# Merge stage: the samples' gather on ScalarE's queue, and a first unit that multiplies its two column halves one after the other

## What is computed

```
xn = rms_norm(x, norm_in)
u = xn @ w_in                                  # columns for both mixers and the merge gates
o_a = rwkv7_mixer(u_a, ...)                    # (tokens, 1024)
o_b = nsa_mixer(q, gates, ...) * silu(g_b)     # (tokens, 1024)
gate_a, gate_b = split(sigmoid(u_m), 2)
merged = gate_a * (o_a @ w_pa) + gate_b * (o_b @ w_pb)
h = x + merged @ w_o
y = rms_norm(h, norm_out)
```

## Time and profile before

| | us |
|---|---|
| median of 3 runs | 2466.56 |
| lowest and highest | 2466.09, 2470.59 |
| the profiled execution, its own time | 2464.72 |
| its span in the profile | 2463.0 |

### The profile page before, as it was taken

How to read it: one execution, slowest core, us unless ns; L and a number is a source line. 1 busy time by engine, 2 the same in 40 slices (tenths; PEclk the granted TensorE clock), 3 DMA queues, 4 the chain that set the end, 5 groups by cost and what they waited for, 6 DMA issues and landing times. The chain is left out here.

```text
span 2463.0 us, 51947 instructions
## 1 busy us (share of the span) xinstructions
PE 2261.5 (92%) x21510; PEld 2082.4 (85%) x21510; DVE 1193.0 (48%) x2352; ACT 803.2 (33%) x1593; POOL 532.9 (22%) x398
## 2 busy tenths in 40 slices
PE   5999999899999989999999789899989869999996
PEld 4998888787888878899999778788987669999996
DVE  4343545445454545368887264444226425353223
ACT  4334233332323332222222345455223214232221
POOL 0000000000000000001100699999604420000000
PEclk8999999999999999999999899999989889999998
DMA  3321112212121121288675412321559955443232
GB/s 114 104 88 50 63 52 71 72 42 71 49 68 50 64 84 51 78 269 282 225 245 181 146 61 83 86 65 55 195 185 307 312 170 181 141 139 128 97 100 82
DMA packets 134590, 302.09 MB, mean 123 GB/s; under 512 B 26442, under 2 KB 54324, under 8 KB 132820
## 3 DMA queue, kind: packets, MB, share of 16 engines
q1 hardware_dynamic: 95236, 208.86, 25.7%
q0 software_dynamic: 15824, 54.71, 6.5%
q10 hardware_dynamic: 23296, 35.20, 4.4%
HBM read 261.48 MB, written 45.54 MB: 125 GB/s over the span
## 5 line engine op out<-in xcount | busy, mean ns | idle before, releaser
L178 PE MATMUL acc<-xh,w_hi 128*128 128x272 f32 x3008 | 675.5, 306 | 42.1 <-DVE w_lo L161 17.9
L178 PE MATMUL acc<-xl,w_hi 128*128 128x272 f32 x3008 | 632.1, 292 | 0.0
L178 PE MATMUL acc<-xh,w_lo 128*128 128x272 f32 x3008 | 631.9, 292 | 0.0
L178 PEld LDWEIGHTS acc<-xh,w_hi 128*128 128x128 f32 x3008 | 479.0, 193 | 101.0 <-issue 53.5
L178 PEld LDWEIGHTS acc<-xl,w_hi 128*128 128x128 f32 x3008 | 484.1, 193 | 0.0
L178 PEld LDWEIGHTS acc<-xh,w_lo 128*128 128x128 f32 x3008 | 481.1, 193 | 0.0
L161 DVE TENSOR_TENSOR w_lo<-w_raw,w_hi 128x1024 fp32r<-128x1024 f32 x164 | 200.6, 1223 | 422.0 <-ACT w_hi L153 421.1
L153 ACT ACTIVATE w_hi<-w_raw 128x1024 fp32r<-128x1024 f32 x188 | 198.4, 1055 | 295.3 <-PE acc L178 220.7
L1265 DVE SCALAR_TENSOR_TENSOR b_C<-b_rows,b_pos_s,b_C 128x512 f32<-128x512 f32 x240 | 162.4, 744 | 0.0
L2618 DVE TENSOR_TENSOR m_w_lo<-m_w,m_w_hi 128x1024 fp32r<-128x1024 f32 x64 | 78.4, 1224 | 164.2 <-ACT m_w_hi L2563 164.1
L970 PEld LDWEIGHTS rbank<-m 64*64 64x64 f32 x3840 | 120.2, 135 | 22.9 <-issue 14.1
(11 more groups left out here) (408 smaller groups left out, 3350.4 us busy)
## 6 DMA issues: line engine op xcount, KB each, us to landing
w_raw<-in_w_all SPq DMA_DIRECT2D x168, 512.0 KB, 3.5
b_rows<-in_cmp_rows SPq DMA_DIRECT2D x128, 256.0 KB, 3.8
m_w<-in_w_mo SPq DMA_DIRECT2D x64, 512.0 KB, 3.9
w_raw<-in_w_all ACTq DMA_DIRECT2D x20, 512.0 KB, 5.9
tmp_uT<-ub ACTq DMA_DIRECT2D x35, 272.0 KB, 4.0
m_gates<-tmp_uT SPq DMA_DIRECT2D x32, 272.0 KB, 2.7
d_ring<-in_sel_k SPq DMA_DIRECT2D x64, 128.0 KB, 4.4
d_ring<-in_sel_k POOLq DMA_DIRECT2D x64, 128.0 KB, 4.6
```

The source lines that it names most:

```text
L178: ins = self.nc.tensor.matmul(acc[:, c, 0:HALF], w[:, k % KH, :], x[:, k, c * HALF:(c + 1) * HALF], start=(k == 0 and m == 0), stop=(k == ...
```

## The change

In `attend_samples`, ACT issues the last store to `obS` ahead of the last two evacuations. In `merge_and_out`, the gather of the samples' `o_a` moves from POOL's to ACT's queue, ahead of the identity. ACT and DVE split the first 8 operand tiles for the 512 prompt columns without waiting for the samples, with weight half 0 first, half 1 ahead of k tile 3 and half 2 ahead of k tile 5; the samples' 32 columns of all 8 tiles are split together at the end. PE's unit 0 does its first column half (columns 0 to 271) over all k tiles, then turns the samples, waits for their low part, and does the second column half (272 to 543).

```diff
--- before.py
+++ after.py
@@ -2187,8 +2187,8 @@
                 out(("Tn", bp), PTn[:, :, :], bank[0:DEC_T, bank_of["Tn", bp], 0:2 * P].rearrange("p (k n) -> p k n", k=2))
                 for n in range(2, N_UNIT):
                     turned(bp, n)
+            store(N_BP - 1)
             background(SAMPLE_PIECES)
-            store(N_BP - 1)
             act.wait_ge(sent, 16 * N_BP)
             for j in range(2):
                 act.wait_ge(stored[j], 16 * ((W.s1 - W.s0 + 1 - j) // 2))
@@ -2534,8 +2534,6 @@
 
         @block.gpsimd
         def _(pool):
-            pool.dma_start(oa_s[:, :].rearrange("n (h d) -> n h d", h=16), A["oS"].rearrange("h n d -> n h d"))\
-                .then_inc(oa_s_in, 16)
             for b in range(DEC_B):
                 src = A["obS"][b // 2, (b % 2) * HD:(b % 2 + 1) * HD, :].rearrange("(g t r) d -> t g (r d)", g=G_KV, t=DEC_T)
                 pool.dma_start(ob_s[b * DEC_T:(b + 1) * DEC_T, :].rearrange("n (g x) -> n g x", g=G_KV), src)\
@@ -2553,6 +2551,8 @@
         @block.scalar
         def _(act):
             f = nc.scalar.activation
+            act.dma_start(oa_s[:, :].rearrange("n (h d) -> n h d", h=16), A["oS"].rearrange("h n d -> n h d"))\
+                .then_inc(oa_s_in, 16)
             act.dma_start(ident[:, :], A["ident"]).then_inc(ident_in, 16)
 
             def high_part(x):
@@ -2567,20 +2567,22 @@
                 f(gates[n % N_RING_M][:, :], gates[n % N_RING_M][:, :], ACT.Sigmoid).then_inc(gated, 1)
 
             def o_high(k):
-                f(o_hi[:, k, :], o_raw[:, k, :], ACT.Copy).then_inc(o_hi_done, 1)
+                cols = slice(0, SEQ if k < KW else NT)
+                f(o_hi[:, k, cols], o_raw[:, k, cols], ACT.Copy).then_inc(o_hi_done, 1)
 
             def square(c):
                 act.wait_ge(added, c + 1)
                 if c >= 2:
                     act.wait_ge(summed, c - 1)
                 f(sq[:, c % 2, :], h[:, c, :], ACT.Square).then_inc(squared, 1)
-            act.wait_ge(taken, 1)
             for k in range(KW):
                 if k % 4 == 0:
                     act.wait_ge(oa_in[k // 4], 16)
+                if k in (0, 3, 5):
+                    high_part((k + 1) // 2 - (k > 0))
                 o_high(k)
-                if k in (1, 3, 5):
-                    high_part((k - 1) // 2)
+            act.wait_ge(taken, 1)
+            f(o_hi[:, 0:KW, SEQ:NT], o_raw[:, 0:KW, SEQ:NT], ACT.Copy).then_inc(o_hi_done, 1)
             for n in range(UNITS):
                 for x in halves_of(n):
                     if n or x > 2:
@@ -2619,8 +2621,10 @@
                     .then_inc(w_lo_done, 1)
 
             def o_low(k):
-                dve.wait_ge(o_hi_done, k + 1)
-                v.tensor_tensor(o_lo[:, k, :], o_raw[:, k, :], o_hi[:, k, :].bitcast(F32), ALU.subtract).then_inc(o_lo_done, 1)
+                dve.wait_ge(o_hi_done, k + 1 if k < KW else k + 2)
+                cols = slice(0, SEQ if k < KW else NT)
+                v.tensor_tensor(o_lo[:, k, cols], o_raw[:, k, cols], o_hi[:, k, cols].bitcast(F32), ALU.subtract)\
+                    .then_inc(o_lo_done, 1)
 
             def silu_half(q):
                 dve.wait_ge(sig, q + 1)
@@ -2659,12 +2663,15 @@
                     merged(n)
                 else:
                     add_residual(n)
+            for k in range(KW):
+                if k in (0, 3, 5):
+                    low_part((k + 1) // 2 - (k > 0))
+                o_low(k)
             dve.wait_ge(tps, 1)
             v.tensor_copy(o_raw[:, 0:KW, SEQ:NT], turn[0][:, 0:KW * NS].rearrange("p (k n) -> p k n", n=NS)).then_inc(taken, 1)
-            for k in range(KW):
-                o_low(k)
-                if k in (1, 3, 5):
-                    low_part((k - 1) // 2)
+            dve.wait_ge(o_hi_done, KW + 1)
+            v.tensor_tensor(o_lo[:, 0:KW, SEQ:NT], o_raw[:, 0:KW, SEQ:NT], o_hi[:, 0:KW, SEQ:NT].bitcast(F32), ALU.subtract)\
+                .then_inc(o_lo_done, 1)
             for n in range(UNITS):
                 for x in halves_of(n):
                     if n or x > 2:
@@ -2717,7 +2724,7 @@
                 j = x % N_RING_M
                 for k in tiles:
                     if ready is not None:
-                        pe.wait_ge(ready, k + 1)
+                        pe.wait_ge(ready[0], k + 1 + ready[1])
                     for m, (a, b) in enumerate(((w_hi, x_hi), (w_hi, x_lo), (w_lo, x_hi))):
                         for c in range(2):
                             ins = mm(out[:, c, 0:HALF], a[j][:, k % KW, :], b[:, k, c * HALF:(c + 1) * HALF],
@@ -2732,9 +2739,23 @@
                              start=(c == 0), stop=(c == N_OUT - 1))
                 ins.then_inc(summed, 1)
             lower, upper = range(KW), range(KW, KD)
-            pe.wait_ge(ident_in, 16)
-            pe.wait_ge(oa_s_in, 16)
-            turn_samples(0, oa_s)
+
+            def first_unit():
+
+                pe.wait_ge(w_lo_done, 1)
+                for c in range(2):
+                    if c:
+                        pe.wait_ge(ident_in, 16)
+                        pe.wait_ge(oa_s_in, 16)
+                        turn_samples(0, oa_s)
+                        pe.wait_ge(o_lo_done, KW + 1)
+                    for k in lower:
+                        if c == 0:
+                            pe.wait_ge(o_lo_done, k + 1)
+                        for m, (a, b) in enumerate(((w_hi, o_hi), (w_hi, o_lo), (w_lo, o_hi))):
+                            ins = mm(acc[0][:, c, 0:HALF], a[0][:, k, :], b[:, k, c * HALF:(c + 1) * HALF],
+                                     start=(k == 0 and m == 0), stop=(k == KW - 1 and m == 2))
+                ins.then_inc(half_done, 1)
             for n in range(UNITS):
                 if n == TURN_AT:
                     pe.wait_ge(ob_s_in, 16 * DEC_B)
@@ -2747,10 +2768,12 @@
                     else:
                         pe.wait_ge(added, n - 1 - 2 * N_OUT)
                 out, x = acc[n % 2], first_half(n)
-                if n < 2 * N_OUT:
-                    half(x, out, lower if n < N_OUT else upper, o_hi, o_lo, True, True, o_lo_done if n in (0, N_OUT) else None)
+                if n == 0:
+                    first_unit()
+                elif n < 2 * N_OUT:
+                    half(x, out, lower if n < N_OUT else upper, o_hi, o_lo, True, True, (o_lo_done, 1) if n == N_OUT else None)
                 else:
-                    ready = m_lo_done if n == 2 * N_OUT else None
+                    ready = (m_lo_done, 0) if n == 2 * N_OUT else None
                     half(x, out, lower, m_hi, m_lo, True, False, ready)
                     half(x + 1, out, upper, m_hi, m_lo, False, True, ready)
                 c = n - 2 * N_OUT - 1
```

## The result

The change made the kernel slower. Over 7 runs each the median went from 2468.43 to 2476.79 us, a ratio of 1.004 (95% interval 1.003 to 1.005), and when it was timed once more beside its parts, from 2469.04 to 2475.91, 1.0034 (1.0022 to 1.0046). That is +8.4 and +6.9 us, where +6.6 was forecast. The median of before was 2466.56 over the three runs shown ahead of the forecast and 2466.6 to 2469.0 in later ones.

What follows compares the result with a forecast made beforehand. PE work bounds the kernel almost everywhere, with full DMA engines limiting the time before unit 0. Unit 0's 10.7 us delay, less 3.9 from the stall and 0.2 from the store, gives +6.6: 2473.2 us, range 2467.5 to 2477.5.

Steps and rivals of the forecast that it cites:

- the first term: Merge's first unit: with its new order, unit 0 ends and unit 1 begins 10.7 us late.
- step 2: Unit 0's first pass: late weight halves delay the operands, so its last three matmuls end at 2039.2.
- A: The forecast itself: late operands, serial turn, second pass at half clock; +6.6 us, range 2470.5 to 2476, chance 0.62.
- the store: End of the samples' stage: the last obS store issued ahead of the evacuations gains 0 to 0.4 us, taken as 0.2.
- Steps 4 and 5: Unit 0 after the turn: samples' copies and subtraction until 2044.1, then 24 matmuls at half clock, 5.4 us, until 2049.6.
- What the stall gives back: Ahead of and in unit 3: PE's 2.4 us idle time and the clock's fall go, returning 3.9 us.
- The gather: Merge start: on ACT's queue ahead of the identity, issue and landing cost nothing, as both are needed only at about 2039.
- Rival B: Unit 0's second pass: the clock is up in time, 3.0 us in place of 5.4; +4.1 us total, chance 0.20.
- A's tail: Unit 0's operands come 1 to 2 us earlier than forecast, so the slowdown stays within 0.2%; chance 0.04.
- same: Whole kernel: the measured time differs from before by no more than about 0.2%, 4.9 us; chance 0.27.
- Rival C: Unit 0's loads: weight half 1 lands sooner, at 2025.0, so the kernel is not slower, 2466.4 us; chance 0.08.
- Rival D: ACT's queue: work behind the samples' copy delays the product unit 2 needs; 2.6 us on the path, +9.2, chance 0.10.

Runs made afterwards that it cites:

- only_first_unit: The change without the moved store and with the gather back on POOL's queue, timed against the kernel before: 2474.02 us, ratio 1.0025.
- change_again: The changed kernel, unaltered, timed once more against the kernel before: 2475.91 us, ratio 1.0034.
- loads_and_gather: The kernel before with SP's two obN loads behind weight half 4 and the samples' gather on ACT's queue: 2464.87 us, ratio 0.9992 to the kernel before.
- fill_gap: The change with 24 useless matmuls ahead of k tile 3 and 6 ahead of k tile 5: 2475.08 us, ratio 1.003 to the kernel before.
- gates_late_warm: The kernel before with later obN and g_b loads, plus 20 useless identity products between the samples' turn and unit 0: 2464.72 us, ratio 0.999.

## Why the prediction came close, and where it was off

- **What failed** is the size of the first term, the 10.7 us by which unit 0 is late: it was 11.6. Most of the miss lies in step 2, the end of the first pass, forecast at 24.6 us from SP's first load and measured at 25.2. Measured 2476.79 lies inside the whole range, but above A's own, 2470.5 to 2476. The rest of the distance to 2473.2 lies outside the merge, in the base and in the start, which the sum gave no room but the 0.2 of the store.
- **The mechanism held, step by step.** PE's first matmul was forecast 3.4 us earlier and came at 12.1 us from SP's first load, before 15.5. It stopped behind the ninth, for 5.5 us. The turn came serially at half clock (3.62 us), then the samples' steps, then 24 matmuls at half clock. only_first_unit has the same late unit 1 and the same merge.
- **The sum.** Unit 1 was forecast 10.7 us late; it came 11.6 late (35.86 less 24.25), and 11.2 in change_again. The missing 0.9 lies in step 2 with 0.6: weight half 2 landed 0.3 later (the forecast allowed such a delay for half 1 and took it as 0), and the last nine matmuls took 2.3 us to the turn's start where 2.0 was reckoned, since the first of them and the change to the turn each take some 0.15 us more than the 0.227 of the others. Steps 4 and 5 add 0.1 each: 1.4 where 1.3 was forecast, and 5.6 where it was 5.5. Measured, the 11.6 is made up of 1.0 (the first pass ends that much later than the whole of unit 0 did), 3.6 for the turn, 1.4 for the samples' steps and 5.6 for the second pass.
- **What the stall gives back**, 3.9 us, held. Unit 1 is 11.6 us late and the prompt's turn ahead of unit 5 is 7.7 late (64.15 from SP's first load, before 56.42), so 3.9 were given back between them. The last 0.26 of the way to 7.5 is the end of the program, which is shorter with the gather off POOL's queue; the forecast had no term for it.
- **The store** brought 0.13 where 0.2 was taken. **The gather** costs nothing in the change, as forecast, since the turn comes only at 25.2 us. But "issue and landing cost nothing" was right only because the turn had moved: alone, the identity behind it made PE's turn 1.4 us late.
- **The base.** +6.6 us was set on a median of 2466.56. Over 7 runs that median was 2468.43. That is 1.9 of the 3.6 us by which 2476.79 lies above 2473.2. The distance between the kernels was short by the other 1.8 us in the first comparison, of which 0.7 is the merge (7.5, forecast 6.8), and by 0.3 in the second. The 1 us outside the merge in the first comparison did not come again; no run separates it from the spread of the start. That the second comparison comes so close to +6.6 is in part luck: unit 0 was 11.2 us late in its profile, the stall gave back 4.1 and the end of the program 0.2, so two misses of a few tenths stand against the first one.
- **A slip in the chances.** With 0.20 for B and 0.04 for A's tail, a sum of 0.27 for "same" has 0.03 of C in it, less than half and not a little more.
- **Rival B** (the clock is up in time) is refuted in its own terms: even with the clock raised on purpose ahead of the turn, it fell before the second pass. In the profile after, the granted clock was 0.50 through all of the first unit, in bursts with waits for loads between them. The rule of the Trainium skill, "TensorE: Matmul & The Clock Gate", section "HAM oscillation — how this bites in real kernels", fits that outcome but is not tested by it: the clock was at 0.50 before the first burst too, so this profile shows bursts that did not raise it, and not a clock that fell back. **Rival C** needed weight half 1 at 10.4 us from SP's first load; it was split at 17.0. **Rival D** did not decide: DVE's product of unit 0 with its gate, for which unit 2 waits, ended at 2057.1, unit 2 began at 2060.94, and PE was busy for 12.20 of the 12.20 us from 2054.90 on.

## What to carry to other kernels

Ask of a reordering which load the last operand of the unit waits for. If the end is set by a load that the change does not move, an early start is spent in waiting, and every step that is taken out of parallel and put behind that last operand (here a turn, three small copies, and half of the matmuls) is paid in full, as the 3.6, 1.4 and 5.6 us show. Look also for the next stall downstream: it hides a part of both gains and losses, and the profile of one kernel shows how much. And in a kernel whose earlier part varies from run to run, count from a landmark behind it.

## What the runs showed of the chip that was not expected

- A small load issued directly behind a gather on the same queue landed much later: the identity (64 KB) took 4.2 us when it was ACT's first DMA, and 8.7 to 9.0 us behind the 128 KB gather in the three profiles read for it.
- How long PE worked at half clock before it rose differed: 5.5 us in unit 0 of before, 3.7 in that of loads_and_gather, and in change_again only the last matmuls of the second pass, some 4.7 us after its start, were at full clock. In fill_gap the clock fell within 1.4 us of idle time behind the turn, and breaks of 1.0 and 0.9 us earlier in the same run had left it up.
- Forty passes of the identity with itself, of no use, brought the clock up 3 us after the first of them in gates_late_warm. They stood right behind the turn's 3.6 us, so what the turn did towards it is not shown.
- The time from the program's start to the merge varied by over 7 us between the profiles, about as much as the whole effect of the change, and all but 0.13 us of it was there before the last samples' result was ready. A length counted from a landmark was the same to 0.01 us within each kind of kernel.
